# x and the first weights in halves of the channels, ahead of the first unit of a hybrid encoder layer

## The reference

```python
x = x + 0.5 * swiglu(rms_norm(x, n_f1), wg1, wu1, wd1)      # 1024 -> 2816 -> 1024
h = rms_norm(x, n_mix) @ w_in                               # three mixers
x = x + jnp.concatenate([y_a, y_b, y_c], axis=-1) @ w_o
x = x + 0.5 * swiglu(rms_norm(x, n_f2), wg2, wu2, wd2)
gate = jax.nn.sigmoid(rms_norm(x, n_ple) @ w_ple_gate)
x = x + gate * (p.astype(x.dtype) @ w_ple_proj)
def swiglu(x, wg, wu, wd):
    return (jax.nn.silu(x @ wg) * (x @ wu)) @ wd
```

## Time and profile before

| | |
|---|---|
| profiled execution, its own time | 1942.22 us |
| its span in the trace | 1940.4 us |
| TensorE busy | 1921.9 us (99%) |
| VectorE busy | 1297.2 us (67%) |
| ScalarE busy | 758.2 us (39%) |
| mean granted clock of TensorE | 0.998 |
| chain that ended last, by engine | PE 89%, DVE 6% |

### The profile page before, as it was taken

The page is one execution under the profiler, slowest core; times in us unless marked ns, Lnnn a source line. Parts: engine busy times, 40 slices in busy tenths (PEclk is TensorE's granted clock), DMA queues, the critical chain, the costliest instruction groups (busy, mean ns, idle before and its releaser), DMA issues.

```text
span 1940.4 us, 36382 instructions
## 1 busy us (share of the span) xinstructions
PE 1921.9 (99%) x14762; PEld 1905.7 (98%) x14762; DVE 1297.2 (67%) x1847; ACT 758.2 (39%) x1076; POOL 82.2 (4%) x63
## 2 busy tenths in 40 slices
PE   8999999999999999999999999999999999999998
PEld 8999999999999999999989999999999999999998
DVE  6966767667886884244446597676677696868634
ACT  7533333334342454021164363333333352434624
POOL 0000000000000002000040100000000000000121
PEclk9999999999999999999999999999999999999999
DMA  5232232325551532111132032323223354541202
GB/s 200 84 104 82 87 133 87 104 82 196 193 201 40 167 115 77 44 34 33 32 128 64 25 111 84 136 89 103 83 82 112 114 200 170 180 153 54 88 22 90
DMA packets 142703, 202.87 MB, mean 105 GB/s; under 512 B 5752, under 2 KB 116048, under 8 KB 139152
## 3 DMA queue, kind: packets, MB, share of 16 engines
q1 hardware_dynamic: 142608, 201.51, 30.8%
HBM read 146.58 MB, written 54.91 MB: 104 GB/s over the span
## 4 chain that ended last, share of the span: by engine, by line
PE 89%; DVE 6%; ACT 1%; issue 1%; DMA 1%; SPq 1%; DVEq 0%; ACTq 0%
PE ps L2781 65%; PE ps L2705 20%; DVE wr_lo L1739 1%; PE ps L2847 1%; DVE xl L2488 1%; PE ps L3067 0%; PE ps L3087 0%; DMA xin_a<-in_x_prompt 0%; PE ps L2962 0%; PE ps L3093 0%; PE ps L3024 0%; PE ps L2730 0%; DVE acc L1718 0%; DVE x L2004 0%; DVE op_lo L1771 0%
## 5 line engine op out<-in xcount | busy, mean ns | idle before, releaser
L2781 PE MATMUL ps<-op_hi,wr_hi 128*128 128x264 f32 x3640 | 742.1, 285 | 3.3 <-DVE sr L1864 1.8
L2781 PE MATMUL ps<-op_lo,wr_hi 128*128 128x264 f32 x3640 | 743.1, 285 | 0.0
L2781 PE MATMUL ps<-op_hi,wr_lo 128*128 128x264 f32 x3640 | 742.2, 285 | 0.0
L2781 PEld LDWEIGHTS ps<-op_hi,wr_hi 128*128 128x128 f32 x3640 | 566.9, 188 | 4.5 <-issue 2.4
L2781 PEld LDWEIGHTS ps<-op_lo,wr_hi 128*128 128x128 f32 x3640 | 565.1, 188 | 0.0
L2781 PEld LDWEIGHTS ps<-op_hi,wr_lo 128*128 128x128 f32 x3640 | 564.8, 189 | 0.0
L1121 ACT ACTIVATE wr_hi<-wr_raw 128x512 fp32r<-128x512 f32 (+1 forms) x268 | 162.3, 617 | 361.2 <-DVE wr_raw L1749 137.0
L2705 PE MATMUL ps<-xh,wh 128*128 128x352 f32 x888 | 196.9, 329 | 1.1 <-DVE tg L2613 0.5
L2705 PE MATMUL ps<-xh,wl 128*128 128x352 f32 x888 | 190.0, 322 | 0.0
L1739 DVE TENSOR_TENSOR wr_lo<-wr_raw,wr_hi 128x512 fp32r<-128x512 f32 (+1 forms) x268 | 173.8, 671 | 22.6 <-ACT wr_hi L1121 17.0
L1121 ACT ACTIVATE wr_hi<-wpair 128x512 fp32r<-128x512 f32 (+1 forms) x201 | 122.7, 615 | 151.3 <-PE ps L2781 137.1
(11 more groups left out here) (318 smaller groups left out, 1680.2 us busy)
## 6 DMA issues: line engine op xcount, KB each, us to landing
h_ops<-hq SPq DMA_DIRECT2D x22, 1848.0 KB, 7.0
op_raw<-h_ops SPq DMA_DIRECT2D x28, 1056.0 KB, 8.4
wpair<-in_w_ffn_up SPq DMA_DIRECT2D x22, 1024.0 KB, 5.4
wpair<-in_w_ffn_gate SPq DMA_DIRECT2D x21, 1024.0 KB, 9.0
wpair<-in_w_ffn_down SPq DMA_DIRECT2D x16, 1024.0 KB, 8.8
wst<-in_w_in SPq DMA_DIRECT2D x22, 512.0 KB, 3.8
op_raw<-h_ops SPq DMA_DIRECT2D x14, 792.0 KB, 4.8
wpair<-in_w_ffn_down SPq DMA_DIRECT2D x8, 768.0 KB, 5.3
```

The source lines that it names most:

```text
L2781: last = pe.matmul(ps[:, out + h, 0:TQ], w_[idx][:, m, :], x_[:, n, h * TQ:h * TQ + TQ], start=idx in (0, 1, 3) and m == 0 and w_ is wr_hi ...
```

## The change

The first five tiles of x are loaded, transposed and copied in two pieces each: the even channel blocks (k = 1) and the odd ones (k = 2), four transposes a piece. A list `PIECES` numbers what is transposed: 0 to 4 even halves of tiles 0 to 4, 5 to 9 their odd halves, 10 to 13 tiles 5 to 8 whole. Each piece has its own place in `X_BANKS`, and `wait_copied` counts pieces. The first 256 weight columns come in four loads, by column half and channel half. The odd halves of x share one semaphore, `x_odd_in`, which is waited for at its full count of five loads; the two odd halves of the weights share `w0_landed[2]`, at its full count of two. The early products are made in the order 0, 2, 1, 3 (`FIRST_MADE`): both that use even channels, then both that use odd ones. The remaining transposes stand at other places between the channel groups. `keep_busy` is new: matmuls of ones by ones whose result is not used, two, three times one, and six of them, between and behind the first five transposes. The two squares of x that ScalarE made between the first copies come later. The diff, cut to its core:

```diff
-    BY_ACT = [1, 3, 5, 7]
+    PIECES = [(t, k) for k in (1, 2) for t in range(HALF_TILES)] + [(t, 0) for t in range(HALF_TILES, NTILE + 1)]
+    BY_ACT = [1, 3, 6, 8, 10, 12]
...
     FIRST_LEFT = ((1, 1), (1, 2), (2, 1), (2, 2))
+    FIRST_MADE = (0, 2, 1, 3)
...
-        X_BANKS = (2, 4, 0, 2, 4, 6, 2, 6, 2)
+        X_BANKS = (2, 3, 4, 5, 6, 2, 3, 6, 7, 3, 6, 2, 6, 2)
...
+        def x_channels(s):
+
+            k = PIECES[s][1]
+            return range(k - 1, KT, 2) if k else range(KT)
...
+            def load_x_channels(t, k):
+                src = a["x_prompt"][0, t * P:t * P + P, :].rearrange("t (m k c) -> t m k c", k=2, c=P)
+                dst = x_tokens(t).rearrange("t (m k c) -> t m k c", k=2, c=P)
+                sp.dma_start(dst[:, :, k - 1, :], src[:, :, k - 1, :]).then_inc(x_in[t] if k == 1 else x_odd_in, 16)
+
             def load_first(n):
 
-                cs = slice((n - 1) * P, n * P)
-                sp.dma_start(wpair[0][:, :, cs], column_tile(ffn_w1[0], cs)).then_inc(w0_landed[n - 1], 16)
-
-            load_x(0)
+                col, k = FIRST_LEFT[n]
+                cs = slice((col - 1) * P, col * P)
+                src = ffn_w1[0][0, :, cs].rearrange("(m k p) n -> p m k n", k=2, p=P)
+                sp.dma_start(wpair[0][:, k - 1:KT:2, cs], src[:, :, k - 1, :]).then_inc(w0_landed[col - 1 if k == 1 else 2], 16)
+
+            load_x_channels(0, 1)
             load_row(*ROWS[0], gain_in)
             for t in range(1, HALF_TILES):
-                load_x(t)
+                load_x_channels(t, 1)
+            load_first(0)
+            load_first(2)
+            for t in range(HALF_TILES):
+                load_x_channels(t, 2)
             load_first(1)
+            load_first(3)
             for t in range(HALF_TILES, NTILE + 1):
                 load_x(t)
-            load_first(2)
...
-            x_square(0)
             x_copy(1)
-            x_square(1)
             x_copy(3)
             first_hi(0)
             act.wait_ge(cols_set, 1)
             wait_copied(act, HALF_TILES)
             for m in range(KP):
                 x_part_hi(0, 0, m)
+            first_hi(2)
+            x_copy(6)
+            x_square(0)
+            x_copy(8)
             first_hi(1)
-            x_copy(5)
+            wait_copied(act, 2 * HALF_TILES)
             for m in range(KP):
                 x_part_hi(0, 1, m)
-            x_copy(7)
-            first_hi(2)
             first_hi(3)
-            wait_copied(act, NTILE + 1)
+            x_copy(10)
+            x_square(1)
+            x_copy(12)
+            wait_copied(act, len(PIECES))
...
             for m in range(KP):
                 x_part_lo(0, 0, m)
+            first_lo(2)
+            x_copy(5)
+            x_copy(7)
+            x_copy(9)
             first_lo(1)
+            wait_copied(dve, 2 * HALF_TILES)
             for m in range(KP):
-                if m == KP // 2:
-                    x_copy(6)
                 x_part_lo(0, 1, m)
-            x_copy(8)
-            first_lo(2)
             first_lo(3)
-            wait_copied(dve, NTILE + 1)
+            x_copy(11)
+            x_copy(13)
+            wait_copied(dve, len(PIECES))
...
-                first_product(0, {1: lambda: x_tile(5), 3: lambda: x_tile(6)})
-                first_product(1, {1: lambda: x_tile(7), 3: lambda: x_tile(8)})
-                first_product(2)
-                first_product(3)
+                def two_pieces():
+
+                    x_transposed(8)
+                    x_transposed(9)
+
+                first_product(0, {1: lambda: x_transposed(5), 2: lambda: x_transposed(6),
+                                  3: lambda: x_transposed(7)})
+                first_product(2, {0: two_pieces})
+                first_product(1, {0: lambda: x_transposed(10), 1: lambda: x_transposed(11),
+                                  3: lambda: x_transposed(12)})
+                first_product(3, {0: lambda: x_transposed(13)})
...
-            def x_tile(t):
-
-                pe.wait_ge(x_in[t], 16)
-                if t == 5:
+            def x_transposed(s):
+
+                t, k = PIECES[s]
+                if k == 2:
+                    pe.wait_ge(x_odd_in, 16 * HALF_TILES)
+                else:
+                    pe.wait_ge(x_in[t], 16)
+                if s == 8:
                     pe.wait_ge(cols_set, 1)
...
+            def keep_busy(n):
+
+                for _ in range(n):
+                    pe.matmul(ps[:, 0, 0:P], ones[:], ones[:], start=True, stop=True)
...
-            x_tile(0)
+            x_transposed(0)
             pe.wait_ge(gain_in, 16)
             rows_as_columns(KT)
-            for t in range(1, HALF_TILES):
-                x_tile(t)
+            keep_busy(2)
+            for s in range(1, HALF_TILES):
+                x_transposed(s)
+                keep_busy(1 if s < HALF_TILES - 1 else 6)
             ffn(0)
```

More of the change, by code:

```diff
@@ L345, in sem @@
             return ctx.enter_context(nc.semaphore(name))
-        w0_landed = [sem(f"w0_landed{b}") for b in range(2)]
+        w0_landed = [sem(f"w0_landed{b}") for b in range(3)]
         wp_landed = [sem(f"wp_landed{b}") for b in range(2)]
@@ L611, in p_ps, with x_ps, x_banks, x_piece @@
             return ps[:, b:b + 2, :]
-        X_BANKS = (2, 4, 0, 2, 4, 6, 2, 6, 2)
-        def x_ps(t):
-            b = X_BANKS[t]
+        X_BANKS = (2, 3, 4, 5, 6, 2, 3, 6, 7, 3, 6, 2, 6, 2)
+        def x_ps(s):
+            b, (t, k) = X_BANKS[s], PIECES[s]
             if t == NTILE:
                 return ps[:, b, 0:KT * dec].rearrange("p (j n) -> p j n", n=dec)
+            if k:
+                return ps[:, b, :].rearrange("p (j n) -> p j n", n=P)
             return ps[:, b:b + 2, :].rearrange("p b (j n) -> p (b j) n", n=P)
+        def x_banks(s):
+            t, k = PIECES[s]
+            return {X_BANKS[s]} if k or t == NTILE else {X_BANKS[s], X_BANKS[s] + 1}
+        def x_channels(s):
+            k = PIECES[s][1]
+            return range(k - 1, KT, 2) if k else range(KT)
+        def x_piece(s):
+            t, k = PIECES[s]
+            return x[:, k - 1:KT:2, rows_of(t)] if k else x[:, :, rows_of(t)]
         def staged(n):
@@ L1054, in x_square @@
                 act.wait_ge(x_in[t], 16)
+                if t < HALF_TILES:
+                    act.wait_ge(x_odd_in, 16 * HALF_TILES)
                 if t > 0:
@@ L2841, in first_product @@
                 ring, xh_, xl_ = FIRST_RING[left], x_op_hi(0, right), x_op_lo(0, right)
-                pe.wait_ge(wop_lo, left + 1)
+                pe.wait_ge(wop_lo, FIRST_MADE.index(left) + 1)
                 for m in range(KP):
@@ L2922, in ffn @@
                     down_unit(f, w)
-            def x_tile(t):
-                pe.wait_ge(x_in[t], 16)
-                if t == 5:
+            def x_transposed(s):
+                t, k = PIECES[s]
+                if k == 2:
+                    pe.wait_ge(x_odd_in, 16 * HALF_TILES)
+                else:
+                    pe.wait_ge(x_in[t], 16)
+                if s == 8:
                     pe.wait_ge(cols_set, 1)
-                earlier = [u for u in range(t) if X_BANKS[u] == X_BANKS[t]]
-                if earlier:
-                    wait_copied(pe, earlier[-1] + 1)
+                in_banks = [v for v in range(s) if x_banks(v) & x_banks(s)]
+                if in_banks:
+                    wait_copied(pe, in_banks[-1] + 1)
                 w = P if t < NTILE else dec
                 src = x_tokens(t)
-                for j in range(KT):
-                    last = pe.transpose(x_ps(t)[:, j, 0:w], src[:, j * P:j * P + P], ident[0:w, 0:w])
+                for i, j in enumerate(x_channels(s)):
+                    last = pe.transpose(x_ps(s)[:, i, 0:w], src[:, j * P:j * P + P], ident[0:w, 0:w])
                 last.then_inc(xt_full, 1)
+            def keep_busy(n):
+                for _ in range(n):
+                    pe.matmul(ps[:, 0, 0:P], ones[:], ones[:], start=True, stop=True)
             def rows_as_columns(n):
```

28 lines of the change are left out of this document (17 added, 11 removed).

## The result

The changed kernel is slower by two thousandths: 1945.28 us median (20 runs, 1942.04 to 1949.14) against 1941.1 (20 runs, 1938.24 to 1943.49), a ratio of 1.0021, 95% interval [1.0015, 1.0027], or +4.2 us (2.9 to 5.2). The forecast was +1.0 with bounds of -1.6 and +5.5; the median lies inside the range given, and the ratio just past the 0.2% at which the text drew the line, on the side that it gave 0.24. The forecast time of 1941.1 was counted from 1940.14, the median of three runs; twenty runs put the kernel before at 1941.1 too, so the forecast is compared here by its shift. The profiled execution took 1943.8 us, with a span of 1942.1.

A forecast was written before the change was run, and what follows sets the result against it. VectorE's packed work behind the last copy of x was taken as the bound: its gain-row copy at L + 20.9 means a shift of L - 13.0, +1.0 us for L = 14.0, on 1940.14 giving 1941.1 us; range 1938.2 to 1945.6.

The forecast's parts named there:

- rival 4: TensorE bounds after all: with VectorE slack behind the last copy of x, the early lead holds; 1935 us, chance 0.05.
- L: Time when all five odd halves of x have landed and their transposes can start; forecast 14.0 us, bounds 11.4 to 18.5.
- Rival 2: Halved x loads move at the slow 212 GB/s, L = 18.5, shift 5.5 us; 1945.6 us, chance 0.20.
- From L to the last copy: TensorE's remaining early products and transposes after L, summed to 13.9 us; last piece of x copied at L + 14.45.
- Behind the last copy: VectorE's stretch up to the gain-row copy: 0.9 us uncovered by ScalarE's high part, then 5.53 of low parts, 6.43 together.
- The late fall: Half clock from 89.8 to 93.2 us, following TensorE's wait of 86.7 to 88.6; forecast to stay.
- rival 3: The late wait moves by 1 us or is split, and no half clock follows: 1.0 - 1.7, 1939.4 us, chance 0.13.
- The first product: TensorE's first product was to start at about 10.5 us, 4.6 sooner than 15.14; window 10 to 11.5.
- The ones: Eleven matmuls of ones keeping TensorE busy between half transposes, costed at nothing; uncovered, up to 2.9 us on the first product's start.
- rival 1: Clock falls early, after 2 us of TensorE idle before L; half speed for 3.4 us, +1.7, 1942.8 us, chance 0.20.
- Rival 5: Each half load pays alone: twelve in series at about 2.9 us put L near 37; end at 1964 us, chance 0.01.
- three signs of being wrong: Sample copy before 25 us; odd wait ending after 16.5; TensorE, not waiting for VectorE up to 54, setting the place of 88.6.

The follow-up runs named there:

- e5_pieces: Kernel before the change, with each of the first five x tiles loaded in two loads of alternate 128-channel blocks (512 B pieces); ratio 1.0014 to the kernel before.
- e6_noones: Changed kernel without its eleven matmuls of ones between the half transposes; ratio 1.0014 to the kernel before the change.

## Why the prediction was right, and where it was off

- *What bounds*: right. VectorE's packed rows from the last copy on decide, with TensorE's products in between (55.1 to 66.5 us in the changed kernel's chain). In the six profiles of the table with no half clock in between and no other wait, the takeover follows the last copy by 61.9 to 62.3 us, with last copies from 23.35 to 29.86. TensorE's lead of 2.6 us at the front was worth nothing, so rival 4 falls.
- *L*: the step that failed in size. I took 14.0, it was 15.5: of the 2.07 us between +1.0 and +3.07, 1.5 are this term. I set the pieces' rate at 308 GB/s for 404, which gives 14.6, and then took the middle between that and 13.4, the value if the slow stretch of 4 to 6 us went. It did go (286 GB/s for 168), but the stretch from 2 to 4 us took its place, with 154 for 346, where I had put the issuing of twice the loads at nothing. From 6 us on, too, the rate was below the one I took: 251 to 300 GB/s in steps of 2 us up to 15.5, where the kernel before had 336 to 408. e5_pieces shows 253 in the mean from 2 to 10 us with the halved loads alone. How much of the 1.5 is the start and how much the rate was not separated. Rival 2 (212 GB/s throughout, L = 18.5) was too dark, but its direction was right. The Trainium skill, "DMA: Bandwidth & Descriptors", "Why small descriptors are slow (HBM only)", says too that each packet carries a fixed overhead, so that short ones are slower, and the trace agrees on the direction: 291 GB/s at a DMA share of 1.19 against 379 at 1.07.
- *From L to the last copy*: 14.36 to its start where I had 14.03. The 0.35 is one wait for the third product's low part, at 22.71, the place where I had written that the cover had nothing to spare.
- *Behind the last copy*: 0.90 idle and 5.71 for 0.9 + 5.53, right.
- *The late fall* stayed, as forecast; rival 3 did not happen in this execution, but where a fall lies is not fixed (below).
- *The first product*: 12.50 for 10.5, outside the 10 to 11.5 that I gave. The first half block was there at 10.2 where I took 7.9, again the rate; it cost nothing, as TensorE then waited 1.3 us for L anyway.
- *The ones and rival 1*: costed at nothing, right as far as the timing tells. Rival 1 did not happen: the early fall did not come, TensorE's two gaps were 1.6 and 1.3 us, with 1.00 behind both; e6_noones shows the fall that the ones hold off.
- *Rival 5* falls: the loads overlap, and the last one took 5.37 us from issue to landing with the queue full ahead of it.
- *The signs and the range*: the first product (12.50), the end of the odd wait (15.50) and the sample copy (29.86) all came later than the windows named for them, and none of the three signs of being wrong appeared. The median's +4.2 is far from the +1.0 of the sum; it lies inside the range because the range went up to the price of rival 2, +5.5, which came to pass only in part. So the path was right, and the range held by its width.
- *What stays open*: the 1.1 us between +3.07 and the median gap of +4.2, which is within its interval. The places come from one execution of each kernel, and the clock's stretch moves between them, so their differences of about 1.5 us hold only where the clock's rows were compared as well.

## What to carry to other kernels

Before work is brought forward, look for the engine that is packed behind it and ask what its first instruction waits for; here that was the last copy of x, and moving four transposes by a few channel groups, with one copy on VectorE, gave a ratio of 0.9985 where bringing the first product forward gave 1.0021. Half loads in pieces of 512 B moved at about three quarters of the rate of whole rows here, and no run tried halves in longer pieces: count what the first half gains against what the whole loses, since the last byte decides. A wait that is removed can come back as a stretch at half the clock, so compare the clock's rows before an experiment is read by one place in the trace.

## What was not expected of the hardware

- In all six profiles without matmuls of ones between the first transposes the granted clock fell to 0.50 within the first 18 us, in three of them behind a wait of 1.8 to 2.1 us for the second tile; in the six with them it held 1.00 up to 48 us or later. Between 45 and 100 us one more stretch at 0.50 came in eleven of the twelve, but not in one place: at 48 to 59 us in five, at 85 to 97 in six. The five are among the six kernels in which TensorE waits 2.4 to 2.8 us for VectorE at 45 to 56 us, and the stretch came right behind that wait; the other six wait at most 0.5 us there for VectorE's low parts, and had none. The same product took 3.15 us outside the stretch and 4.42 to 4.69 inside.
- The DMA share does not tell the rate: at 0.90 from 2 to 10 us, 328 GB/s in rows of 4 KB and 253 in pieces of 512 B; from 12 to 14 us 404 GB/s at 1.02 before the change, and 291 at 1.21 after it.
- A half load, in four pieces a row, took SP 0.65 us to issue (2.60 for four), a whole one 0.45 (1.78 for four).
